# Column constants inside the turned x, a later first norm, and identity products ahead of the first matmul

## What is computed

```
def rms_norm(x, g):
    xf = x.astype(jnp.float32)
    y = xf * lax.rsqrt(jnp.mean(xf * xf, axis=-1, keepdims=True) + EPS) * g.astype(jnp.float32)
    return y.astype(x.dtype)
...
        h = rms_norm(x, norm_mix[l])
        proj = h @ w_in[l]
        aq, ak, av, rq, rk, rv, rg, ga, gr = jnp.split(proj, offsets, axis=-1)
```

## Time and profile before

| | |
|---|---|
| median of 3 runs | 1201.28 us (1200.06 to 1201.92) |
| the profiled execution's own time | 1199.97 us |
| its span, first to last instruction | 1197.9 us |
| PE busy | 1054.1 us (88%) |
| DVE busy | 805.4 us (67%) |
| ACT busy | 613.2 us (51%) |
| POOL busy | 327.0 us (27%) |
| first TensorE instruction | 9.58 us into the span |

### The profile page before, as it was taken

The page is one execution under the profiler, slowest core; times in us unless marked ns, Lnnn a source line. Parts: engine busy times, 40 slices in busy tenths (PEclk is TensorE's granted clock), DMA queues, the critical chain, the costliest instruction groups (busy, mean ns, idle before and its releaser), DMA issues.

```text
span 1197.9 us, 12629 instructions
## 1 busy us (share of the span) xinstructions
PE 1054.1 (88%) x3792; PEld 660.2 (55%) x3792; DVE 805.4 (67%) x1678; ACT 613.2 (51%) x1347; POOL 327.0 (27%) x287
## 2 busy tenths in 40 slices
PE   6999999999999999898889998877768777788787
PEld 5788878888878777684445444423323222333232
DVE  4763667665545688667597787766776677667754
ACT  6464554554445467645555655445444434543453
POOL 1000000100000000025345444554544454445441
PEclk9999999999999999999999999999999999989999
DMA  8463346966535764339999999999999999999996
GB/s 317 142 199 117 129 126 241 304 196 190 175 105 176 246 193 159 132 122 412 416 420 422 420 421 422 420 422 422 417 422 414 423 419 422 410 408 422 422 418 278
DMA packets 95684, 369.53 MB, mean 308 GB/s; under 512 B 6592, under 2 KB 30152, under 8 KB 62992
## 3 DMA queue, kind: packets, MB, share of 16 engines
q0 software_dynamic: 38464, 273.46, 55.4%
q1 hardware_dynamic: 57168, 95.44, 23.8%
HBM read 367.81 MB, written 1.06 MB: 308 GB/s over the span
## 4 chain that ended last, share of the span: by engine, by line
DMA 22%; PE 17%; DVE 14%; issue 3%; ACT 2%; POOL 1%; DVEq 0%; ACTq 0%
DMA uv_ring<-in_peer_uv,expert 22%; PE gemm L1987 13%; DVE uv_ring L1473 5%; POOL uv_ring L472 1%; DVE hit L1463 1%; DVE hit L1461 1%; DVE picked L1464 1%; ACT diag L891 1%; PE gemm L1573 1%; PE gemm L1575 1%; PE gemm L1574 1%; DVE pos L1436 1%; DVE best L1426 1%; DVE best L1433 1%; DVE cand_rest L1430 1%
## 5 line engine op out<-in xcount | busy, mean ns | idle before, releaser
L1987 PE MATMUL gemm<-uv_ring,diag 128*128 128x512 f32 x1024 | 494.0, 625 | 114.1 <-ACT diag L891 113.7
L1473 DVE CUSTOM_DVE_ANT_0 uv_ring<-uv_ring,xn 128x1024 f32<-128x1024 f32 x256 | 309.7, 1221 | 151.5 <-DMA uv_ring<-in_peer_uv,expert 149.7
L1987 PEld LDWEIGHTS gemm<-uv_ring,diag 128*128 128x128 f32 x1024 | 189.9, 196 | 393.1 <-ACT diag L891 223.3
L472 POOL DMA_INDIRECT uv_ring<-in_peer_uv,expert x256 | 310.3, 1212 | 336.8 <-PE gemm L1987 311.0
L933 DVE TENSOR_TENSOR w_lo<-raw,w_hi 128x1024 fp32r<-128x1024 f32 (+1 forms) x184 | 193.1, 1061 | 147.1 <-ACT w_hi L499 146.6
L499 ACT ACTIVATE w_hi<-raw 128x1024 fp32r<-128x1024 f32 (+1 forms) x184 | 168.6, 927 | 180.5 <-PE gemm L1575 178.3
L1573 PE MATMUL gemm<-w_hi,hT_hi 128*128 128x512 f32 (+1 forms) x592 | 244.0, 412 | 13.1 <-DVE w_lo L933 13.0
L1575 PE MATMUL gemm<-w_hi,hT_lo 128*128 128x512 f32 (+1 forms) x592 | 228.9, 387 | 0.0
L1574 PE MATMUL gemm<-w_lo,hT_hi 128*128 128x512 f32 (+1 forms) x592 | 228.5, 386 | 0.0
L885 ACT ACTIVATE hid_g<-hid,scales 128x1 f32<-128x1 f32 x256 | 75.0, 293 | 298.1 <-DVE hid L1473 296.5
L1573 PEld LDWEIGHTS gemm<-w_hi,hT_hi 128*128 128x128 f32 x592 | 112.1, 189 | 42.0 <-DVE w_lo L933 14.4
(11 more groups left out here) (244 smaller groups left out, 850.7 us busy)
## 6 DMA issues: line engine op xcount, KB each, us to landing
raw<-in_w_in SPq DMA_DIRECT2D x31, 1024.0 KB, 5.1
raw<-in_w_gate SPq DMA_DIRECT2D x22, 512.0 KB, 4.0
raw<-in_w_up SPq DMA_DIRECT2D x22, 512.0 KB, 4.9
raw<-in_w_down SPq DMA_DIRECT2D x22, 512.0 KB, 3.3
raw<-in_w_out SPq DMA_DIRECT2D x8, 1024.0 KB, 5.0
raw<-in_peer_w_query SPq DMA_DIRECT2D x8, 1024.0 KB, 6.3
uv_ring<-in_peer_uv,expert POOLq DMA_INDIRECT x258, 13.5
raw<-in_w_ret_o SPq DMA_DIRECT2D x4, 1024.0 KB, 5.2
```

What stands on the lines that cost most here:

```text
L472: nc.gpsimd.indirect_dma_start(out=uv_ring[k % RING][:, 0:(2 * D if whole else D)], out_offset=None, in_=peer_uv, in_offset=bass.IndirectO ...
L1473: V.tensor_tensor_reduce(out=u_row, in0=u_row, in1=xn[:, b, :], scale=1.0, scalar=0.0, op0=ALU.mult, op1=ALU.add, accum_out=hid[par][:, k: ...
L1987: last = nc.tensor.matmul(gemm[2 * b + n][:], diag[k % 4][:], uv_ring[k % RING][:, D + n * CHUNK:D + (n + 1) * CHUNK], start=(begin and k ...
```

## The change

- The gain and other column constants (26 columns, padded to 32) are put by the host ahead of turned x in the same array. The first DMA of turned x brings them along, and the DMA of their own is gone. `xn` and `gains` become views of one tile `gains_xT`.
- Turned x comes in three pieces (2, 2 and 4 k tiles) in place of two (2 and 6); the second weight quarter of chunk 0 is issued ahead of the last piece.
- Chunk 1's loads are issued ahead of the two halves of x.
- POOL's two small loads wait until the second half of chunk 0 has landed.
- On ACT and on DVE the split of chunk 1 stands ahead of the first norm (squares, root, inverse).
- TensorE, once the identity is made, multiplies the identity by itself 24 times (`WARM`) into a bank that nobody reads, ahead of chunk 0.

```diff
-            sp.dma_start(gains[:], gain_cols).then_inc(gains_landed, 16)
-
             def load_xt(piece, k, n):
-                sp.dma_start(xT[:, k:k + n, :], x_t[:, k:k + n, :]).then_inc(xt_landed[piece], 16)
+                cols = slice(G_COLS + k * S if k else 0, G_COLS + (k + n) * S)
+                sp.dma_start(gains_xT[:, cols], x_t[:, cols]).then_inc(xt_landed[piece], 16)
...
+            pool.wait_ge(w_landed[0][1], 16)
             pool.dma_start(rel_ext[:, 127:127 + REL], rel_bias_2[0]).then_inc(rel_loaded, 16)
...
-            act.wait_ge(gains_landed, 16)
             for q in range(4):
-                if q < 2:
+                if q < 3:
                     act.wait_ge(xt_landed[q], 16)
...
                 hi(None, 0, landed(0), quarters=(q,))
+            hi_at(1, n=512)
             for b in range(TB):
                 act.wait_ge(x_landed[b], 16)
                 for half in range(2):
                     squares(b, half)
             root("norm1", TB)
-            hi_at(1, n=512)
             scaled("norm1", 1)
...
                 lo(None, 0, quarters=(q,))
+            lo_at(1, n=512)
             dve.wait_ge(squared, SQUARES["norm1"] + 4)
...
-            lo_at(1, n=512)
...
+            pe.wait_ge(ident_made, 1)
+            for n in range(WARM):
+                nc.tensor.matmul(trb[0][:, 0:P], ident[:], ident[:], start=True, stop=True)
             product_at(0, ready=first_columns)
-            pe.wait_ge(ident_made, 1)
```

More of the change, by code:

```diff
@@ L8, in two_block_kernel @@
 def two_block_kernel(
-    nc, x, x_t, gain_cols, w_in, att_sinks, w_att_o, w_ret_o, w_out, norm_ffn, w_gate, w_up, w_down,
+    nc, x, x_t, w_in, att_sinks, w_att_o, w_ret_o, w_out, norm_ffn, w_gate, w_up, w_down,
     final_norm, ln_mix_g_2, w_in_2, gmlp_norm_g_2, gmlp_ws_t, rel_bias_2,
@@ L86, in two_block_kernel @@
     SCORE_JOBS = [(0, 0, 4), (0, 4, 4), (1, 0, 2), (1, 2, 2), (1, 4, 2), (1, 6, 2)]
-    G_RET, G_BS, G_Q, G_K, G_MIX, G_COLS = 0, 8, 16, 17, 18, 26
+    G_RET, G_BS, G_Q, G_K, G_MIX, G_COLS = 0, 8, 16, 17, 18, 32
     SC_MIX, SC_AQ, SC_FFN, SC_FINAL, SC_IN2, SC_PEER, SC_COLS = 0, 2, 4, 6, 8, 10, 12
@@ L94, in two_block_kernel @@
     APART = TOPK - 2
+    WARM = 24
     ctx = ExitStack()
@@ L120, in two_block_kernel @@
         x_sb = sb("x_sb", [P, TB, D])
-        xn = sb("xn", [P, TB, D])
+        gains_xT = sb("gains_xT", [P, G_COLS + TB * D])
+        gains = gains_xT[:, 0:G_COLS]
+        xn = gains_xT[:, G_COLS:G_COLS + TB * D].rearrange("p (b d) -> p b d", b=TB)
         hT = [sb("hT_hi", [P, KD, S], f32r), sb("hT_lo", [P, KD, S], f32r)]
@@ L163, in two_block_kernel @@
         ident = sb("ident", [P, P])
-        gains = sb("gains", [P, G_COLS])
         scales = sb("scales", [P, SC_COLS])
@@ L223, in two_block_kernel @@
         x_landed, ident_made = [sem("x_landed0"), sem("x_landed1")], sem("ident_made")
-        gains_landed, aux_landed, sinks_landed = sem("gains_landed"), sem("aux_landed"), sem("sinks_landed")
+        aux_landed, sinks_landed = sem("aux_landed"), sem("sinks_landed")
         ffn_landed, late_landed = sem("ffn_landed"), sem("late_landed")
-        xt_landed, w_first = [sem("xt_landed0"), sem("xt_landed1")], sem("w_first")
+        xt_landed, w_first = [sem(f"xt_landed{i}") for i in range(3)], sem("w_first")
         xt_hi, xt_split, scale_ready, ws_masked = sem("xt_hi"), sem("xt_split"), sem("scale_ready"), sem("ws_masked")
@@ L331, in _ @@
             load_first(0, w_first)
-            load_xt(1, 2, 6)
+            load_xt(1, 2, 2)
             load_first(2, w_landed[0][0])
+            load_xt(2, 4, 4)
             def half_free(c, half):
@@ L363, in _ @@
             load(0, 0, w_in[0], 0, halves=(1,))
+            load(1, 1, w_in[0], AK, width=256)
             for b in range(TB):
                 load_x(b)
-            load(1, 1, w_in[0], AK, width=256)
             with sp.Fori(0, 5) as i:
@@ L2021, in _ @@
             add_rows(1, PEER_HEADS - 1, end=True)
-NAMES = ["x", "x_t", "gain_cols", "w_in", "att_sinks", "w_att_o", "w_ret_o", "w_out", "norm_ffn", "w_gate", "w_up", "w_down",
+NAMES = ["x", "x_t", "w_in", "att_sinks", "w_att_o", "w_ret_o", "w_out", "norm_ffn", "w_gate", "w_up", "w_down",
          "final_norm", "ln_mix_g_2", "w_in_2", "gmlp_norm_g_2", "gmlp_ws_t", "rel_bias_2",
@@ L2036 @@
     laid["peer_uv"] = np.concatenate([np.asarray(inputs["peer_u_2"])[0], np.asarray(inputs["peer_v_2"])[0]], axis=1)
-    laid["x_t"] = np.asarray(inputs["x"])[0].reshape(256, 8, 128).transpose(2, 1, 0)
     laid["gmlp_ws_t"] = np.asarray(inputs["gmlp_w_s_2"])[0].transpose(2, 0, 1)
     head_gains = [np.pad(np.asarray(inputs[name]), ((0, 0), (0, 64))) for name in ("q_norm_g_2", "k_norm_g_2")]
-    laid["gain_cols"] = np.concatenate([np.asarray(inputs["ret_gn_gain"]).reshape(8, 128), np.asarray(inputs["gmlp_b_s_2"])[0], *head_gains,
-                                        np.asarray(inputs["norm_mix"]).reshape(8, 128)], axis=0).T
+    gain_cols = np.concatenate([np.asarray(inputs["ret_gn_gain"]).reshape(8, 128), np.asarray(inputs["gmlp_b_s_2"])[0], *head_gains,
+                                np.asarray(inputs["norm_mix"]).reshape(8, 128)], axis=0).T
+    x_t = np.asarray(inputs["x"])[0].reshape(256, 8, 128).transpose(2, 1, 0).reshape(128, 2048)
+    laid["x_t"] = np.concatenate([np.pad(gain_cols, ((0, 0), (0, 6))), x_t], axis=1)
     nc = bacc.Bacc("TRN2", target_bir_lowering=False, num_devices=1)
```

## The result

The changed kernel takes 1204.45 us in the median of 16 runs (1203.34 to 1206.93), the kernel before 1201.12 (1199.53 to 1203.60, 16 runs): a ratio of 1.0027, with a 95% interval of 1.0020 to 1.0034, so 3.3 us or 0.27% slower. The profiled execution took 1204.45 us itself, its span 1202.4.

A forecast was written before the change was run, and what follows sets the result against it. The start was taken to bound it: whatever delays TensorE's beginning of chunk 2 delays the end equally. Front -1.2 plus squares and norm behind chunk 0's end +4.2 gave +3.0 on 1201.28: 1204.3 us, range 1201.2 to 1207.0.

The forecast's parts named there:

- the shift at chunk 2 isn't the shift at 540 us: Sign of a wrong prediction: the delay when chunk 2 starts, forecast +3.0 us, differs from the delay when the gathers start.
- ACT's chain: ACT from chunk 0's end through quarter split, squares, norm and taking out: forecast 6.19 us, against 1.98 before.
- a hole: TensorE ahead of turning the query heads: forecast to stand from 23.8 to 27.1 us, a new stop of 3.3 us.
- The front: Kernel start up to chunk 0's end: forecast to end at 20.9 us against 22.12, a gain of 1.2 us.
- What follows comes 0.45 us earlier: First loads: one issue fewer on SP's queue brings the first low part from 8.30 to 7.85 us.
- That costs nothing: POOL's two small loads, some 10 us later: claimed free, as their first reader comes after the query heads.
- all engines have the same shift: Everything from chunk 2 on: claimed to move by the same amount as chunk 2's start, forecast +3.0 us.
- rival 2: TensorE's clock falls in its stop before the query heads and stays low into chunk 2: +0.5 to +1.7 us; chance 0.12.
- the slack of 1.7 us: Ahead of chunk 2: TensorE's own work done at 31.0 us, chunk 2 forecast to begin at 32.75.
- Rival 3: Part given back later: the half-rate stretch at 504 us, costing 1.7 us, may not come, giving 1202.6 us; chance 0.14.
- Rival 1: Identity products at the start don't lift the clock, or overrun to 11.9 us; chunk 0 ends 3.6 later, 1207.9 us; chance 0.07.
- Rival 4: Not slower: the squares don't wait for chunk 0's end, leaving a shift of -1.2 us, 1200.1 us; chance 0.07.

## Why the prediction was right

**The whole.** 1204.3 us was forecast, +3.0, and 1204.45 was measured, +3.3, in the range and on the side that had 0.71. The mechanism held, but one of the prediction's own signs of being wrong came true: "if the shift at chunk 2 isn't the shift at 540 us". It was 2.45 us at chunk 2 and 4.05 at the first gather.

**The mechanism and its size.** That the squares would stand behind the end of chunk 0, that ACT's chain from there would take 6.2 us to the turning of the query heads and TensorE only 2.87, and that chunk 2 would begin 11.85 us after chunk 0's end, all came nearly as written: 6.35 us from chunk 0's end to the turning (26.70 - 20.35) for 6.2, a hole of 3.33 us for 3.3, chunk 2 at 32.21 - 20.35 = 11.86 in the changed kernel and 11.85 with the late norm alone. Put back, the hole was gone. These terms were sums of measured rows on one engine's fixed order, and they held.

**The front was mis-sized, by half a microsecond, out of three errors.** "What follows comes 0.45 us earlier" was the term that failed: the constants' own transfer had delayed the next one by more than its issue, so the first `w_lo` came at 6.23 and not at 7.85. "That costs nothing", of the small loads, was wrong too: it priced their readers, not what they do to the transfers beside them, and the third quarter gained 1.17 us where only 0.45 was counted. And the identity products took 7.7 us for 7.4; since the first operand was there at 7.5, they were not hidden behind it but held chunk 0 up by 1.8 us. What set the forecast end was the third quarter, which came 0.72 us sooner than forecast; the products, as they ended at 9.33, took back 0.17 of that. Chunk 0 ran from 9.33 without a wait and ended at 20.35, 0.55 ahead of the forecast of 20.9. So chunk 2 came at +2.45 and not at +3.0.

**What wasn't seen at all.** The part of the change that merges two tiles also moves the split buffers by 128 bytes, and the down product lost 1.3 us by it, two shorter products some 0.4 more. The prediction said of everything behind chunk 2 that "all engines have the same shift". Without this the shift at the first gather would have been nearer 2.4 us than 4.05. The forecast's agreement to 0.15 us in the median is in part luck: a front taken 0.55 too late, a missing 1.7, and a median that shows 3.3 us where the two profiled executions differ by 4.5.

**The rivals.** Of rival 2 (half rate after the hole, lasting into chunk 2) the first half took place, from 27.04 on, but not the second: chunk 1 had ended just when chunk 2's first operand came, as the slack of 1.7 us allowed. In the kernels without identity products or with the small loads early it did reach on, for 0.6 to 0.9 us. The Trainium skill ("TensorE: Matmul & The Clock Gate", HAM oscillation) says that an idle gap beyond some length puts the clock back to half. The changed kernel's trace agrees: 3.3 us of standing, and the granted clock at 0.55 after. So do four of the other five with this stop; with the late norm alone the clock held after 3.31 us. Rival 3 (something given back at 504) didn't occur in the changed kernel, whose stretch came at 508.32 and cost the same; but the kernel with the place alone put right shows that the other sign is possible too: it got a second one. Rival 1 (they end at 11.9 and leave the clock low) didn't occur: they ended at 9.33, 0.3 us later than forecast, and by the windows of the changed kernel the products took 0.21 us a record and then 0.11 (4.90 us over 23, 2.80 over 26), so they did lift the clock:

```profile
1.60:6.50 4.90, 4.90 (x23) 1.00 0.93 295
6.50:9.30 2.80, 2.80 (x26) 1.00 1.01 368
```

Rival 4 (the front gain stays) didn't occur: the squares did wait for the end of chunk 0.

## What to carry to other kernels

Work that hides behind another engine's product must stay ahead, in its own queue, of whatever waits for that product's end; moving it behind such a wait adds all of it to that queue's path (4.2 us here, of which TensorE stood 3.3), and the size of this can be summed up from the rows of one timeline before anything is run. Warming an engine up is worth only what its first real work isn't waiting for anyway: here 24 identity products put off chunk 0's start by nearly as much as the faster clock saved, and bought 0.2 us at its end (in the median of the changed kernel, where the hole follows, 1.4 to 2.6 us); with 12, chunk 0 waited for its third quarter instead. And a change of a tile's size or place is an edit to everything allocated behind it: compare the step of the long products, not only the part of the program that was edited.

## What the runs showed of the hardware

- A move of the split weights by 128 bytes against the activations that they are multiplied with made TensorE's step in the down product 0.232 us instead of 0.227 at the same granted clock of 1.00 (61.1 to 61.4 us against 59.7 to 59.8 over 261 steps, seven traces each). Two other products of 512 columns whose operands moved against each other show it too (0.228 to 0.232 and 0.233); where both operands moved together the step stayed at 0.228. Why the place matters was not tried.
- A transfer of 13 KB at the head of the queue cost the next one 1.6 us from issue to landing (4.3 against 2.7 us). Two small loads of 12 KB together, on POOL's queue, delayed a 1 MB weight load beside them by 1.9 us (14.23 against 12.30 us; 11.95 to 12.53 in the kernels where they wait).
- 24 fp32 products of 128 columns show as 48 records; chunk 0 could start 7.7 to 8.1 us after the first of them. Half as many took 4.9 us. In the view of the windows the granted clock reads 1.00 there from the start, though the steps (0.21 us, then 0.11) show both levels: the view has no value until the clock's first recorded change, so at a kernel's start the steps are to be read.
- Begun without such products, chunk 0 ran at half rate for 3.0 to 4.6 us (seven traces): 3.3 in the kernel before and 4.6 in the one with only the column constants moved, whose instructions are the same.
- A half-rate stretch began in or within 1.2 us after the stop of 3.3 us in five of the six traces that have it, after that of 3.0 us in twelve of fourteen, and after that of 1.7 to 2.3 us in seven of fourteen. Two of them instead of one between the down product and the output product went with 1.6 us more.
